# Three attention stages of a two-block transformer kernel: the first scores inside the last projection, transposes four steps behind the scores

## The chip, the core and the metric

The kernel is one program on one core of a Trainium2 chip. The time is the device time of one execution in microseconds (us); the median of the runs of the kernel before is 2651.66 us. The engines are TensorE (PE, with its weight loads as PEld), VectorE (DVE), ScalarE (ACT), GpSimd (POOL) and SyncE (SP, which issues the loads). They run side by side, each in its own program order, and meet through semaphores.

## The reference, cut to what matters

Two blocks run over 512 tokens of width 1024 (16 heads of 64). The change touches three attention stages, called a, b and c here:

```
a: logits = q k / 8 over the keys that an index picked     (causal by blocks)
b: logits = q k / 8 + decay[query] - decay[key]            (causal)
c: logits = norm(q) norm(k) / 8                            (all keys)
p  = softmax(logits)        o = p v        x = x + o @ w_o
```

Around them stand projections (`x @ w_q` and the like), MLPs and a gated MLP, all in float32.

## The kernel before

**Stages.** Everything runs as one chain of matrix products on PE, a projection as tiles of one PSUM bank each (128x512 or 128x256), in banks 0 to 3 in turn. A product splits the operands into a high and a low part and adds three matmuls for each piece (lines 452 to 454, for `va` and `vc` 475 to 477). ACT and POOL split the weights of the next 256 columns ahead of time (`split`, lines 900 and 1706), SP loads them. Between products and the next norm ACT and DVE evacuate each tile. All orders are written out by hand, engine by engine.

**An attention.** There are 32 steps, `STEPS = (c, i)`: pair of heads c (8 of them), query block i (4). In a and b step i is 128(i+1) keys wide, in c always 512. So four steps make a group of a pair. A step n passes these operations:

1. PE, line 584 (in b also 592, for the decay): the scores of the two heads, into banks `2 * (n % 2) + e`.
2. DVE, line 1329 (c: 1327): takes them out of PSUM with the mask and the minimum, into a row of `PA`/`PBB`/`PC` (8 rows, `ROWS`, two for a step).
3. ACT, line 991: exponential and its sum.
4. DVE, line 1342: reciprocal of the two sums; DVE does it for step n - 1 after it has taken the scores of step n.
5. POOL, line 1740, and DVE, line 1345: each row times its reciprocal. Of the even steps DVE takes one row and POOL one, of the odd steps POOL takes both.
6. PE, line 609, `turn`: transposes of both rows into banks 4 and 5; all steps use these two banks, so a turn waits until the copies of the turn before are out.
7. ACT, line 985, and DVE, line 1336: copies of banks 4 and 5 to `TA`/`TB`/`TC` (of the even steps one each, of the odd steps both on ACT).
8. PE, line 624, `values`: the product with v, into bank 6 or 7; after each group ACT and DVE (lines 995, 1349) take it out as the input of the output projection.

The loop over n does the scores of step n, then the turn of step n - 3 (`TURN`), then the values of step n - 5 (`SUM`). Each engine has the same loop with its own share, so what stands ahead in an engine's order delays what stands behind it. ACT does, in its turn n, first the copies of turn n - 3 and then the exponentials of step n; DVE the scores of step n, the copy of turn n - 3, the reciprocals of step n - 1.

**Before and behind.** The first scores wait until the last projection (`va`, `qb`, `vc`) is through and its four banks are free (`wait_bank` of the tiles `end + i`). The products `oa`, `ob`, `oc` follow the last values. The last projection of b, `qb`, has eight tiles of 24 matmuls, that of c, `vc`, four tiles of 24 half as wide.

Of the kernel before, what the change touches and what calls it, by code (L numbers as in the profile page):

```python
# [19 lines left out]

ROWS, TURN, SUM = 8, 3, 5
BIG = 1e30
# [94 lines left out]
def body(nc, ctx, t, consts, out):  # L117
# [223 lines left out]
    def by_heads(x, w):  # L341

        return x.rearrange("p (e k) -> p e k", e=2)[:, :, 0:w // 2]

    def scaled_by(a, n):

        return 16 * ATT[a] + n // 2 + 1, 48 * ATT[a] + n + 1 + (n + 1) // 2

# [39 lines left out]
    def freed(g):  # L388
        return FREED[g]

    def tensor_program(pe):
# [180 lines left out]

        def attend(a, heads_q, heads_k, heads_v):

            base, x0 = 64 * ATT[a], fill_base(a + "o")[1]

            def scores(n):
                c, i = STEPS[n]
                w = width(a, i)  # L580
                for e in range(2):
                    if n >= 2:
                        pe_until.wait_ge(sc_out, base + 2 * n + e - 3)
                    m = pe.matmul(bank[2 * (n % 2) + e][:, 0:w], heads_q(2 * c + e, i), heads_k(2 * c + e, w), start=True, stop=(a != "b"))  # L584
                    if a != "b":
                        m.then_inc(sc_full, 1)
                if a == "b":

                    for e in range(2):  # L590
                        o, h = 64 * e, 2 * c + e
                        pe.matmul(bank[2 * (n % 2) + e][:, 0:w], PICK[o:o + 64, h:h + 1].to_broadcast([64, P]), CK[o:o + 64, 0:w],
                                  start=False, stop=True).then_inc(sc_full, 1)
# [33 lines left out]

            for n in range(len(STEPS) + SUM):
                if n < len(STEPS):
                    scores(n)  # L630
                if TURN <= n < len(STEPS) + TURN:
                    turn(n - TURN)
                if n >= SUM:
                    values(n - SUM)

# [70 lines left out]
        pe_until.wait_ge(key_copy, 4)  # L706
        for i in range(4):
            wait_bank(GEMM["va"].end + i)
        attend("a",
               lambda h, i: QA[64 * (h % 2):64 * (h % 2) + 64, h // 2, i * P:(i + 1) * P],  # L710
               lambda h, w: KA[h // 4][64 * (h % 2):64 * (h % 2) + 64, 0:w],
               lambda h, j: VA[:, j, 64 * (h // 4):64 * (h // 4) + 64])
        fm("oa", X, lambda c: wait_chunk("ao", c))
# [43 lines left out]
        tm_wide("vb", lambda c: wait_chunk("kv", c), after_vb)  # L757
        fm("qb", X, lambda c: wait_chunk("qb", c), first=lambda c: wait_high("qb", c))
        pe_until.wait_ge(ck_dve, 7)
        for i in range(4):  # L760
            wait_bank(GEMM["qb"].end + i)
        attend("b",
               lambda h, i: QB[64 * (h % 2):64 * (h % 2) + 64, h // 2, i * P:(i + 1) * P],
               lambda h, w: KB[64 * (h % 2):64 * (h % 2) + 64, h // 2, 0:w],
               lambda h, j: VB[:, j, 64 * h:64 * h + 64])
        fm("ob", X, lambda c: wait_chunk("bo", c))
# [40 lines left out]
        pe_until.wait_ge(rot_sum, 17)  # L807
        pe_until.wait_ge(key_copy, 8)
        for i in range(4):
            wait_bank(GEMM["vc"].end + i)  # L810
        attend("c",
               lambda h, i: QC[64 * (h % 2):64 * (h % 2) + 64, h // 2, i * P:(i + 1) * P],
               lambda h, w: KCC[h // 4][64 * (h % 2):64 * (h % 2) + 64, 0:w],
               lambda h, j: VC[:, j, 64 * (h // 4):64 * (h // 4) + 64])
        fm("oc", X, lambda c: wait_chunk("co", c))
# [70 lines left out]
    def scalar_program(act):  # L886
# [86 lines left out]

        def attend(a):
            base = 64 * ATT[a]
            for n in range(len(STEPS) + SUM + 1):
                if TURN <= n < len(STEPS) + TURN:
# [180 lines left out]
        def evac_vc(o):  # L1158
# [54 lines left out]
    def vector_program(dve):  # L1213
# [98 lines left out]
        def attend(a, mask):  # L1312
            base, hi0 = 64 * ATT[a], fill_base(a + "o")[0]
            for n in range(len(STEPS) + SUM + 1):
                if n < len(STEPS):
                    i = STEPS[n][1]
                    w = width(a, i)
                    for r in (2 * n, 2 * n + 1):
                        p, st = PROBS[a][r % ROWS], stat[:, r % ROWS, :]
                        b = bank[2 * (n % 2) + r % 2]  # L1320
                        dve_until.wait_ge(sc_full, base + r + 1)
# [15 lines left out]
                if 1 <= n < len(STEPS) + 1:  # L1337
# [359 lines left out]
    def gpsimd_program(pool):  # L1697
# [230 lines left out]
```

## Time and profile before

| | |
|---|---|
| median of 3 runs (lowest, highest) | 2651.66 us (2650.67, 2652.53) |
| the profiled execution | 2654.48 us, its span 2653.2 us |
| busy share of the span, PE / DVE / ACT / POOL | 97% / 49% / 37% / 47% |
| attention a, first scores to the first matmul of `oa` | 147.0 to 224.2 us |
| attention b, first scores to the last values | 783.3 to 861.6 us |
| attention c, first scores to the last values | 1365.8 to 1460.5 us |

PE is busy almost throughout, and the chain of work that ended last lies on it for 84% of the span; so a microsecond in which PE waits, or runs at a lower clock, is a microsecond of the time. A row of the timeline gives start, duration, engine, line, what is written and read, count, and in brackets how long the engine stood idle before and what ended that. Matmul durations overlap their neighbours' (a matmul's start to the next one's start is what it costs). A row of groups gives count, busy us, mean ns of one and idle time before; a row by line gives count: ns least/median/most, first and last start. PEclk is the granted TensorE clock as a share of its full 2.4 GHz; 0.50 is 1.2 GHz.

### The profile page before, as it was taken

What the parts mean: (1) busy time and instruction counts of PE and PEld (TensorE: products, weight loads), DVE (VectorE), ACT (ScalarE), POOL (GpSimd) and SP (SyncE); (2) the same over time, 40 slices, a digit from 0 to 9 for tenths busy, and PEclk for the clock granted to TensorE, in tenths of its full rate; (3) what the DMA queues carried; (4) which work ended last, traced back from release to release, by engine and by line L of the source; (5) the groups of instructions that cost most, each with busy time, mean ns of one, the idle gap of its engine ahead of it and who ended that gap; (6) DMA issues with size and microseconds to landing.
All of it is one profiled execution on the core that took longest, in us unless ns stands there. A gap on an engine that the chain in (4) does not pass through costs nothing.

```text
span 2653.2 us, 33052 instructions
## 1 busy us (share of the span) xinstructions
PE 2579.4 (97%) x13418; PEld 2084.4 (79%) x13418; DVE 1288.4 (49%) x2151; ACT 979.5 (37%) x1620; POOL 1255.2 (47%) x618
## 2 busy tenths in 40 slices
PE   8989999999998999999999999999999999999999
PEld 5667888888776888888766888888788888888887
DVE  4863799842035399992557341222345233431221
ACT  4464423223347332232458342232324222432231
POOL 4865444444447444444468344444343444344442
PEclk9999999999999999999999999999999999999999
DMA  4201555532220366552210233322432222333322
GB/s 145 64 17 49 181 188 182 188 117 75 95 80 2 95 196 198 186 165 96 72 49 2 64 111 96 95 95 80 163 96 83 81 94 80 95 96 95 96 96 79
DMA packets 259436, 274.48 MB, mean 103 GB/s; under 512 B 6869, under 2 KB 249301, under 8 KB 259029
## 3 DMA queue, kind: packets, MB, share of 16 engines
q1 hardware_dynamic: 259284, 272.37, 31.9%
q8 instruction: 106, 1.74, 0.3%
q14 instruction: 46, 0.37, 0.0%
HBM read 270.26 MB, written 2.10 MB: 103 GB/s over the span
## 4 chain that ended last, share of the span: by engine, by line
PE 84%; DVE 8%; POOL 4%; issue 2%; ACT 1%; DMA 0%; SPq 0%; DVEq 0%
PE bank L452 22%; PE bank L453 22%; PE bank L454 22%; DVE acc L1362 2%; PE bank L520 2%; PE bank L522 2%; PE bank L521 2%; PE bank L428 2%; PE bank L429 2%; DVE tmp L1397 2%; PE bank L432 2%; POOL PA L1740 1%; POOL PBB L1740 1%; PE bank L584 1%; PE bank L624 1%
## 5 line engine op out<-in xcount | busy, mean ns | idle before, releaser
L1706 POOL TENSOR_TENSOR wlo<-raw,whi 128x1024 fp32r<-128x1024 f32 (+1 forms) x408 | 988.8, 2445 | 1193.9 <-ACT whi L900 1193.8
L452 PE MATMUL bank<-Xhi,whi 128*128 128x512 f32 (+1 forms) x1616 | 640.4, 396 | 1.4 <-POOL wlo L1706 1.4
L453 PE MATMUL bank<-Xlo,whi 128*128 128x512 f32 (+1 forms) x1616 | 629.9, 390 | 0.0
L454 PE MATMUL bank<-Xhi,wlo 128*128 128x512 f32 (+1 forms) x1616 | 629.1, 389 | 0.0
L900 ACT ACTIVATE whi<-raw 128x1024 fp32r<-128x1024 f32 (+1 forms) x408 | 404.9, 1041 | 570.0 <-PE bank L454 495.6
L452 PE MATMUL bank<-Hhi,whi 128*128 128x512 f32 x1024 | 400.6, 391 | 0.0
L453 PE MATMUL bank<-Hlo,whi 128*128 128x512 f32 x1024 | 398.9, 390 | 0.0
L454 PE MATMUL bank<-Hhi,wlo 128*128 128x512 f32 x1024 | 398.4, 389 | 0.0
L452 PEld LDWEIGHTS bank<-Xhi,whi 128*128 128x128 f32 (+1 forms) x1616 | 302.3, 187 | 73.0 <-issue 8.1
L453 PEld LDWEIGHTS bank<-Xlo,whi 128*128 128x128 f32 (+1 forms) x1616 | 302.4, 187 | 65.0 <-issue 3.2
L454 PEld LDWEIGHTS bank<-Xhi,wlo 128*128 128x128 f32 (+1 forms) x1616 | 302.4, 187 | 65.0
L1362 DVE SCALAR_TENSOR_TENSOR acc<-ada,cond,acc 128x256 f32<-128x256 f32 x336 | 272.6, 811 | 12.0
L1265 DVE SCALAR_TENSOR_TENSOR HT<-bank,MOD,HT 128x512 f32<-128x512 f32 (+1 forms) x99 | 72.2, 734 | 404.3 <-PE bank L454 384.9
L1397 DVE TENSOR_TENSOR tmp<-tmp 128x512 f32<-128x512 f32 x128 | 137.2, 1072 | 235.4 <-ACT tmp L1007 235.4
L1007 ACT ACTIVATE tmp<-bank 128x512 f32<-128x512 f32 x128 | 76.6, 598 | 412.6 <-PE bank L454 400.3
L454 PEld LDWEIGHTS bank<-Hhi,wlo 128*128 128x128 f32 x1024 | 192.3, 188 | 40.3
L452 PEld LDWEIGHTS bank<-Hhi,whi 128*128 128x128 f32 x1024 | 192.2, 188 | 39.9
L453 PEld LDWEIGHTS bank<-Hlo,whi 128*128 128x128 f32 x1024 | 192.3, 188 | 39.1
L1263 DVE TENSOR_TENSOR HT<-bank,HT 128x512 f32<-128x512 f32 (+1 forms) x84 | 54.7, 663 | 167.2 <-PE bank L454 167.2
L1400 DVE TENSOR_TENSOR Hlo<-tmp,Hhi 128x512 fp32r<-128x512 f32 x128 | 120.8, 944 | 14.0 <-DVE tmp L1397 0.9
L943 ACT ACTIVATE held<-HT 128x512 f32<-128x512 f32 (+1 forms) x56 | 32.0, 578 | 178.0 <-DVE HT L1263 103.2
L520 PE MATMUL bank<-whi,Xhi 128*128 128x512 f32 x240 | 94.7, 395 | 0.5 <-POOL wlo L1706 0.5
(269 smaller groups left out, 3146.6 us busy)
## 6 DMA issues: line engine op xcount, KB each, us to landing
ada<-in_ada_w SPq DMA_DIRECT2D x48, 1024.0 KB, 5.3
raw<-in_w_up SPq DMA_DIRECT2D x32, 1024.0 KB, 5.7
raw<-in_w_down SPq DMA_DIRECT2D x32, 1024.0 KB, 5.0
raw<-in_mlp_w_in SPq DMA_DIRECT2D x32, 1024.0 KB, 5.6
raw<-in_mlp_w_out SPq DMA_DIRECT2D x32, 1024.0 KB, 5.2
raw<-in_gmlp_w_in SPq DMA_DIRECT2D x24, 1024.0 KB, 5.0
raw<-in_gmlp_w_out SPq DMA_DIRECT2D x12, 1024.0 KB, 5.0
raw<-in_w_in_a SPq DMA_DIRECT2D x8, 1024.0 KB, 5.2
```

Of the source, the lines that this page charges most:

```text
L452: pe.matmul(b[0:rows, :], whi[s][:, c, j:j + rows], hi[:, c, :], start=(c == 0), stop=False)
L453: pe.matmul(b[0:rows, :], whi[s][:, c, j:j + rows], lo[:, c, :], start=False, stop=False)
L454: m = pe.matmul(b[0:rows, :], wlo[s][:, c, j:j + rows], hi[:, c, :], start=False, stop=(c == KC - 1))
L520: pe.matmul(b[:], Xhi[:, c, q * P:(q + 1) * P], hi[:, k, :], start=(c == 0), stop=False)
L900: act.activation(whi[u % 2][:, c0:c1, 0:k], src[:, c0:c1, 0:k], ACT_F.Copy).then_inc(hi_done, 1)
L1007: act.activation(tmp[v % 2][:], bank[(gm.tile + o) % 4][:], ACT_F.Relu).then_inc(up_q, 1)
L1263: d = dve.tensor_tensor(HT[:, o, at], b[:, at], HT[:, o, at], ALU.add)
L1265: d = dve.scalar_tensor_tensor(HT[:, o, at], b[:, at], gate[:, o:o + 1], HT[:, o, at], ALU.mult, ALU.add)
L1362: dve.scalar_tensor_tensor(a[:], src[:, c, :], cd[:, c:c + 1], a[:], ALU.mult, ALU.add).then_inc(ada_step, 1)
L1397: dve.tensor_tensor(r[:], tmp[v % 2][:], tmp[v % 2][:], ALU.mult).then_inc(up_r, 1)
L1400: dve.tensor_tensor(Hlo[g % 2][:, o, :], r[:], Hhi[g % 2][:, o, :].bitcast(F32), ALU.subtract).then_inc(h_lo, 1)
L1706: pool.tensor_tensor(wlo[u % 2][:, c0:c1, 0:k], src[:, c0:c1, 0:k], whi[u % 2][:, c0:c1, 0:k].bitcast(F32), ALU.subtract).then_inc(lo_done, 1)
```

## The change

`TURN` becomes 4 and `SUM` 6: a step is transposed one step later, its values follow one step later, and the loop has one turn more. `ROWS` becomes 10, so that the probability rows last as long; for the room, six buffers of the index stage before attention a (`RL`) now share the space of `TA`. The scores of steps 0 to 3 go to banks 4 to 7, which no projection tile uses; steps 4 and 5 wait for the projection's last tiles in their banks, and turn 0 and values 0 wait until banks 4 to 7 have been read. In b, steps 0 to 3 stand behind tiles 4 to 7 of `qb`, one each; in c, steps 0 and 1 behind tile 2 of `vc` and steps 2 and 3 behind tile 3. ACT's order changes with it; DVE's and POOL's loops only see `TURN` and `SUM`. In a nothing stands between tiles, but the first scores no longer wait for the tiles of `va`. Of the scaling, now the even steps are POOL's with both rows and the odd ones are shared.

```diff
-ROWS, TURN, SUM = 8, 3, 5
+ROWS, TURN, SUM = 10, 4, 6
-        RL = [sb(f"RL{i}", [P, S], F32, region) for i in range(8)]
+        RL = [TA[i // 2][:, i % 2, :] for i in range(6)] + [sb(f"RL{i}", [P, S], F32, region) for i in range(6, 8)]
+    def score_bank(n, e):
+        return (4 if n < TURN else 0) + 2 * (n % 2) + e
...
             def scores(n):
-                    if n >= 2:
+                    if TURN <= n < TURN + 2:
+                        pe_until.wait_ge(*freed(end - 4 + (score_bank(n, e) - end) % 4))
+                    elif n >= 2:
                         pe_until.wait_ge(sc_out, base + 2 * n + e - 3)
             def turn(n):
-                pe_until.wait_ge(pn_dve, by_dve)
+                if n:
+                    pe_until.wait_ge(pn_dve, by_dve)
+                else:
+                    pe_until.wait_ge(sc_out, base + 6)
             def values(n):
+                if n == 0:
+                    pe_until.wait_ge(sc_out, base + 8)
...
-        for i in range(4):
-            wait_bank(GEMM["va"].end + i)
...
+        def after_qb(o):
+            if o == 4:
+                pe_until.wait_ge(ck_dve, 7)
+                pe_until.wait_ge(*freed(GEMM["qb"].tile))
+            if o >= 4:
+                steps_b(o - 4, o - 3)
+        steps_b(4)
         def after_vc(o):
+            if o == 2:
+                pe_until.wait_ge(rot_sum, 17)
+                pe_until.wait_ge(key_copy, 8)
+                pe_until.wait_ge(qn_root, 1)
+                steps_c(0, 2)
+            if o == 3:
+                steps_c(2, 4)
+        steps_c(4)
...
+        def evac_qb(o):
+            keep_heads("qb", QB)(o)
+            if o >= 4:
+                attend("b", o - 4, o - 3)
-                    if n % 2:
+                    if n % 2 == 0:
                         dve_until.wait_ge(rc_done, base // 2 + n)
                         dve.tensor_scalar(p[:, 0:w], p[:, 0:w], both[:, 0, 2:3], None, ALU.mult).then_inc(pn_dve, 1)
-                for r in (2 * n, 2 * n + 1)[1 - n % 2:]:
+                for r in (2 * n, 2 * n + 1)[n % 2:]:
                     pool.tensor_scalar(p[:, 0:w], p[:, 0:w], st[:, 2:3], None, ALU.mult).then_inc(pn_pool, 1)
```

PE at the end of `qb`, before: the last matmul of the last tile, then the scores (`KB,QB` and, for the decay, `CK,PICK`) of steps 0 to 3, the first turn (`ident,PBB`), and the scores of step 4.

```order
L454 MATMUL bank<-Xhi,wlo 128x512
L584 MATMUL bank<-KB,QB 128x128 x2
L592 MATMUL bank<-CK,PICK 128x128 x2
L584 MATMUL bank<-KB,QB 128x256 x2
L592 MATMUL bank<-CK,PICK 128x256 x2
L584 MATMUL bank<-KB,QB 128x384 x2
L592 MATMUL bank<-CK,PICK 128x384 x2
L584 MATMUL bank<-KB,QB 128x512 x2
L592 MATMUL bank<-CK,PICK 128x512 x2
L609 MATMUL bank<-ident,PBB 128x64 x4
L584 MATMUL bank<-KB,QB 128x128 x2
```

The same place of the changed kernel, from the last matmul of the last tile on (its lines are 5 to 14 further down).

```order
L459 MATMUL bank<-Xhi,wlo 128x512
L595 MATMUL bank<-KB,QB 128x512 x2
L603 MATMUL bank<-CK,PICK 128x512 x2
L595 MATMUL bank<-KB,QB 128x128 x2
L603 MATMUL bank<-CK,PICK 128x128 x2
L623 MATMUL bank<-ident,PBB 128x64 x4
L595 MATMUL bank<-KB,QB 128x256 x2
```

Steps 0 to 2 have gone ahead of it, behind tiles 4, 5 and 6, so only step 3 stands between the last tile and step 4, and the first turn stands behind step 4.

ACT over the last tiles of `qb`, before: the split of weights (`whi<-raw`), two evacuations, then the exponentials (`PBB,stats`) and the first copies of a turn (`TB`).

```order
L900 ACTIVATE whi<-raw 128x1024 x2
L1098 ACTIVATE QB<-bank 128x512 x2
L900 ACTIVATE whi<-raw 128x1024 x2
L1098 ACTIVATE QB<-bank 128x512 x2
L991 ACT_TABLE_LOAD
L991 ACTIVATE PBB,stats<-PBB,stats 128x128 x2
L991 ACTIVATE PBB,stats<-PBB,stats 128x256 x2
L991 ACTIVATE PBB,stats<-PBB,stats 128x384 x2
L985 ACTIVATE TB<-bank 128x2x64
```

The same in the changed kernel.

```order
L926 ACTIVATE whi<-raw 128x1024 x2
L1124 ACTIVATE QB<-bank 128x512
L1017 ACT_TABLE_LOAD
L1017 ACTIVATE PBB,stats<-PBB,stats 128x128 x2
L1124 ACTIVATE QB<-bank 128x512
L1017 ACTIVATE PBB,stats<-PBB,stats 128x256 x2
L926 ACTIVATE whi<-raw 128x1024 x2
L1124 ACTIVATE QB<-bank 128x512
L1017 ACTIVATE PBB,stats<-PBB,stats 128x384 x2
L1124 ACTIVATE QB<-bank 128x512
L1017 ACTIVATE PBB,stats<-PBB,stats 128x512 x2
L1011 ACTIVATE TB<-bank 128x2x64
```

Each evacuation of tiles 4 to 7 has the exponentials of one step behind it, the split of the first weights of `ob` stands behind the exponentials of step 1, and the first copy of a turn behind those of step 3.

POOL at the start of attention b, before: the last weight split, then one row of step 0 (128 wide), both of step 1, one of step 2, both of step 3, one of step 4.

```order
L1706 TENSOR_TENSOR wlo<-raw,whi 128x1024 x8
L1740 TENSOR_SCALAR PBB<-PBB,stats 128x128
L1740 TENSOR_SCALAR PBB<-PBB,stats 128x256 x2
L1740 TENSOR_SCALAR PBB<-PBB,stats 128x384
L1740 TENSOR_SCALAR PBB<-PBB,stats 128x512 x2
L1740 TENSOR_SCALAR PBB<-PBB,stats 128x128
```

The same in the changed kernel.

```order
L1738 TENSOR_TENSOR wlo<-raw,whi 128x1024 x8
L1772 TENSOR_SCALAR PBB<-PBB,stats 128x128 x2
L1772 TENSOR_SCALAR PBB<-PBB,stats 128x256
L1772 TENSOR_SCALAR PBB<-PBB,stats 128x384 x2
L1772 TENSOR_SCALAR PBB<-PBB,stats 128x512
L1772 TENSOR_SCALAR PBB<-PBB,stats 128x128 x2
```

In a and b POOL has lost one of the two widest rows of a group and has both of the 384 wide ones; the number of rows is the same.

## Rows read from the trace of the kernel before

**Rows 1.** PE's waits for POOL in a, b, c: total us, times, longest.

```profile
PE bank L609 <- POOL PA L1740: 8.5, 9, 2.1
...
PE bank L609 <- POOL PBB L1740: 7.5, 9, 2.1
...
PE bank L609 <- POOL PC L1740: 8.7, 9, 1.8
```

**Rows 2.** Timeline of PE, one group of four steps of a (steps 8 to 11).

```profile
162.59 0.49 PE L584 MATMUL bank<-KA,QA 64*128 64x128 f32 x4
163.42 0.47 PE L609 MATMUL bank<-ident,PA 64*128 64x64 f32 x8 [0.34 <-DVE TA L1336]
...
168.05 0.71 PE L609 MATMUL bank<-ident,PA 64*128 64x64 f32 x16 [0.93 <-POOL PA L1740]
...
171.26 0.49 PE L584 MATMUL bank<-KA,QA 64*128 64x128 f32 x4
```

**Rows 3.** Timeline of PE, one group of b (steps 8 to 11).

```profile
798.20 0.49 PE L584 MATMUL bank<-KB,QB 64*128 64x128 f32 x4
...
799.03 0.46 PE L609 MATMUL bank<-ident,PBB 64*128 64x64 f32 x8 [0.28 <-DVE TB L1336]
...
803.66 0.71 PE L609 MATMUL bank<-ident,PBB 64*128 64x64 f32 x16 [0.64 <-POOL PBB L1740]
...
807.11 0.49 PE L584 MATMUL bank<-KB,QB 64*128 64x128 f32 x4
```

**Rows 4.** Timeline of PE, two groups of c (scores of steps 8, 12, 16).

```profile
1384.15 1.13 PE L584 MATMUL bank<-KC,QC 64*128 64x512 f32 x4
...
1394.44 1.13 PE L584 MATMUL bank<-KC,QC 64*128 64x512 f32 x4
1396.29 0.71 PE L609 MATMUL bank<-ident,PC 64*128 64x64 f32 x16 [0.72 <-POOL PC L1740]
...
1405.68 1.13 PE L584 MATMUL bank<-KC,QC 64*128 64x512 f32 x4
```

**Rows 5.** Timeline of PE, the first scores of a, b, c.

```profile
147.04 4.41 PE L584 MATMUL bank<-KA,QA 64*128 64x128 f32 x16 [3.38 <-ACT VA L1081]
...
783.30 0.46 PE L584 MATMUL bank<-KB,QB 64*128 64x128 f32 x3 [0.78 <-ACT QB L1098]
...
1365.82 5.18 PE L584 MATMUL bank<-KC,QC 64*128 64x512 f32 x16 [0.56 <-ACT VC L1164]
```

**Rows 6.** Timeline of PE: last scores (step 31), then `oa` or the last values.

```profile
212.65 1.13 PE L584 MATMUL bank<-KA,QA 64*128 64x512 f32 x4
...
224.17 0.50 PE L452 MATMUL bank<-Xhi,whi 128*128 128x512 f32 x1
...
849.45 1.13 PE L584 MATMUL bank<-KB,QB 64*128 64x512 f32 x4
...
857.77 3.85 PE L624 MATMUL bank<-TB,VB 128*64 128x128 f32 x36
...
1448.03 1.13 PE L584 MATMUL bank<-KC,QC 64*128 64x512 f32 x4
...
1457.70 2.84 PE L624 MATMUL bank<-TC,VC 128*64 128x128 f32 x48
```

**Rows 7.** Windows: length, busy PE, PEld, DVE, ACT, POOL (count), PEclk, DMA.

```profile
155.00:160.00 5.00, 4.83 (x38) 2.79 (x36) 2.07 (x8) 2.76 (x8) 4.45 (x5) 0.50 0.00 0
...
170.00:180.00 10.00, 8.73 (x116) 6.09 (x114) 6.72 (x28) 8.48 (x29) 8.29 (x8) 1.00 0.01 2
...
790.00:795.00 5.00, 4.83 (x46) 3.49 (x46) 3.14 (x12) 2.70 (x11) 3.88 (x5) 0.50 0.01 3
```

**Rows 8.** Durations: an exponential of c; POOL's scaling, b by form, c by line.

```profile
1368.57 0.70 ACT L991 ACTIVATE PC<-PC,stats 128x512 f32<-128x512 f32 x1
...
L1740 POOL TENSOR_SCALAR PBB<-PBB,stats 128x384 f32<-128x384 f32 x8 | 11.6, 1454 | 6.1 <-DVE stats L1342 6.1
...
L1740 POOL TENSOR_SCALAR PC<-PC,stats x48: 1560/1566/1859, 1370.0 to 1455.4; 128x512 f32<-128x512 f32 x48
```

More of the change, by code:

```diff
@@ L343, in by_heads @@
         return x.rearrange("p (e k) -> p e k", e=2)[:, :, 0:w // 2]
+    def score_bank(n, e):
+        return (4 if n < TURN else 0) + 2 * (n % 2) + e
     def scaled_by(a, n):
-        return 16 * ATT[a] + n // 2 + 1, 48 * ATT[a] + n + 1 + (n + 1) // 2
+        return 16 * ATT[a] + (n + 1) // 2, 48 * ATT[a] + n + 2 + n // 2
     def turned_by(a, r):
@@ L572, in rotation, with attention @@
             pe.matmul(bank[4][0:rows, :], perm[p][0:rows, 0:rows], rotated(r)[0:rows, :], start=True, stop=True).then_inc(rot_full, 1)
-        def attend(a, heads_q, heads_k, heads_v):
+        def attention(a, last, heads_q, heads_k, heads_v):
             base, x0 = 64 * ATT[a], fill_base(a + "o")[1]
+            end = GEMM[last].end
             def scores(n):
@@ L581, in scores @@
                 for e in range(2):
-                    if n >= 2:
+                    if TURN <= n < TURN + 2:
+                        pe_until.wait_ge(*freed(end - 4 + (score_bank(n, e) - end) % 4))
+                    elif n >= 2:
                         pe_until.wait_ge(sc_out, base + 2 * n + e - 3)
-                    m = pe.matmul(bank[2 * (n % 2) + e][:, 0:w], heads_q(2 * c + e, i), heads_k(2 * c + e, w), start=True, stop=(a != "b"))
+                    m = pe.matmul(bank[score_bank(n, e)][:, 0:w], heads_q(2 * c + e, i), heads_k(2 * c + e, w), start=True, stop=(a != "b"))
                     if a != "b":
@@ L591, in scores @@
                         o, h = 64 * e, 2 * c + e
-                        pe.matmul(bank[2 * (n % 2) + e][:, 0:w], PICK[o:o + 64, h:h + 1].to_broadcast([64, P]), CK[o:o + 64, 0:w],
+                        pe.matmul(bank[score_bank(n, e)][:, 0:w], PICK[o:o + 64, h:h + 1].to_broadcast([64, P]), CK[o:o + 64, 0:w],
                                   start=False, stop=True).then_inc(sc_full, 1)
@@ L626, in values, with steps @@
                 m.then_inc(pv_done, 1)
[L628 to L634, printed above, removed]
+            def steps(first, to=len(STEPS) + SUM):
+                for n in range(first, to):
+                    if n < len(STEPS):
+                        scores(n)
+                    if TURN <= n < len(STEPS) + TURN:
+                        turn(n - TURN)
+                    if n >= SUM:
+                        values(n - SUM)
+            return steps
         pe_until.wait_ge(ident_in, 16)
@@ L706, in tensor_program @@
         pe_until.wait_ge(key_copy, 4)
-        for i in range(4):
-            wait_bank(GEMM["va"].end + i)
[L709 to L712, printed above, removed]
+        attention("a", "va",
+                  lambda h, i: QA[64 * (h % 2):64 * (h % 2) + 64, h // 2, i * P:(i + 1) * P],
+                  lambda h, w: KA[h // 4][64 * (h % 2):64 * (h % 2) + 64, 0:w],
+                  lambda h, j: VA[:, j, 64 * (h // 4):64 * (h // 4) + 64])(0)
         fm("oa", X, lambda c: wait_chunk("ao", c))
@@ L757, in tensor_program @@
         tm_wide("vb", lambda c: wait_chunk("kv", c), after_vb)
[L758 to L765, printed above, removed]
+        steps_b = attention("b", "qb",
+                            lambda h, i: QB[64 * (h % 2):64 * (h % 2) + 64, h // 2, i * P:(i + 1) * P],
+                            lambda h, w: KB[64 * (h % 2):64 * (h % 2) + 64, h // 2, 0:w],
+                            lambda h, j: VB[:, j, 64 * h:64 * h + 64])
+        def after_qb(o):
[4 more added lines that the diff above has]
+                steps_b(o - 4, o - 3)
+        fm("qb", X, lambda c: wait_chunk("qb", c), after_qb, first=lambda c: wait_high("qb", c))
+        steps_b(4)
         fm("ob", X, lambda c: wait_chunk("bo", c))
@@ L800, in tensor_program @@
         fm("qc", X, lambda c: wait_chunk("c", c), after_qc)
+        steps_c = attention("c", "vc",
+                            lambda h, i: QC[64 * (h % 2):64 * (h % 2) + 64, h // 2, i * P:(i + 1) * P],
+                            lambda h, w: KCC[h // 4][64 * (h % 2):64 * (h % 2) + 64, 0:w],
+                            lambda h, j: VC[:, j, 64 * (h // 4):64 * (h // 4) + 64])
         def after_vc(o):
@@ L805, in after_vc @@
                 rotation(ROT_C_AT["q", 7], 1)
-        tm("vc", lambda c: wait_chunk("c", c), after_vc)
[L807 to L814, printed above, removed]
+            if o == 2:
[5 more added lines that the diff above has]
+                steps_c(2, 4)
+        tm("vc", lambda c: wait_chunk("c", c), after_vc)
+        steps_c(4)
         fm("oc", X, lambda c: wait_chunk("co", c))
@@ L972, in copy_keys, with attend @@
                 act.activation(k[64:128, :], k[0:64, :], ACT_F.Copy).then_inc(key_copy, 1)
-        def attend(a):
+        def attend(a, first=0, to=len(STEPS) + SUM + 1):
             base = 64 * ATT[a]
-            for n in range(len(STEPS) + SUM + 1):
+            for n in range(first, to):
                 if TURN <= n < len(STEPS) + TURN:
@@ L1123, in scalar_program @@
         fill("qb", None, GEMM["vb"].end)
-        units("qb", keep_heads("qb", QB))
-        attend("b")
+        def evac_qb(o):
+            keep_heads("qb", QB)(o)
+            if o >= 4:
+                attend("b", o - 4, o - 3)
+        units("qb", evac_qb)
+        attend("b", 4)
         units("ob", lambda o: square("ob", GEMM["ob"].tile + o, o))
@@ L1164, in evac_vc @@
             act.activation(VC[:, o, :], bank[g % 4][:, 0:256], ACT_F.Copy).then_inc(copied, 1)
+            if o == 2:
+                attend("c", 0, 2)
         units("vc", evac_vc)
-        attend("c")
+        attend("c", 2)
         units("oc", lambda o: square("oc", GEMM["oc"].tile + o, o))
@@ L1319, in attend @@
                         p, st = PROBS[a][r % ROWS], stat[:, r % ROWS, :]
-                        b = bank[2 * (n % 2) + r % 2]
+                        b = bank[score_bank(n, r % 2)]
                         dve_until.wait_ge(sc_full, base + r + 1)
```

## The prediction

> **What bounds the kernel now.** The chain of waits lies on PE for 84% of the span, so I looked only for time that PE loses in a, b and c: by waiting, or at a lower clock. The list of PE's waits came first: in each attention PE waits nine times for POOL before a turn, 24.7 us in all [rows 1]. The timelines then show three kinds of places.
>
> *The middle* (steps 8 to 31, six groups). A group of a takes 171.26 - 162.59 = 8.67 us, of which PE waits 0.34 for DVE's copy of the turn before and 0.93 for POOL, so its work is 7.4 [rows 2]. A group of b takes 8.91, waits 0.28 + 0.64 = 0.92, work 8.0 [rows 3]. In c four steps without a wait take 10.29, the next four 11.24, so one wait of 0.72 costs 0.95 [rows 4]; five such follow steps 8 to 31. Clock: 1.00 there, with ACT busy 8.48 of 10 us in a [rows 7].
>
> *The head* (end of the last projection tile to the scores of step 8). In b it runs from 783.30 - 0.78 = 782.52 to 798.20, 15.7 us [rows 3, 5]; in a from 143.66 to 162.59, 18.9 [rows 2, 5]; in c from 1365.26 to 1384.15, 18.9 [rows 4, 5]. PE's work in a head is eight scores, turns 0 to 4, values 0 to 2. Start to next start, a group's work (the 13, 18 and 12 rows between the first and last of rows 2, 3 and the first two of rows 4) splits into scores 2.9, 3.5, 3.9; turns 1.7, 1.7, 2.4; values 2.8, 2.8, 4.1 for a, b, c. That makes 5.8 + 1.9 + 1.8 = 9.5 (a), 7.0 + 1.9 + 1.8 = 10.7 (b), 7.8 + 2.9 + 3.1 = 13.8 (c). Lost: 9.4, 5.0, 5.1. Part of it in a and b is the clock at 0.50 behind the idle stretches [rows 7].
>
> *The tail* (scores of step 31 to the last values): 11.5, 12.2 and 12.5 us [rows 6]. Its work is one score, four turns, six values: 1.0 + 1.7 + 4.6 = 7.3; 1.2 + 1.7 + 4.6 = 7.5; 1.0 + 2.4 + 6.1 = 9.5. Lost: 4.2, 4.7, 3.0.
>
> **The change part by part.** It takes no matmul away. Each score, turn and value still costs PE the same, wherever it stands; what can be won is lost time, 9.4 + 5.0 + 5.1, 7.6 + 5.5 + 4.75, and 4.2 + 4.7 + 3.0, together 49. So I ask at each place what is late next.
>
> *Middle.* A turn one step later gives the chain behind the scores (DVE, ACT, DVE, POOL) one more step, 1.85 to 2.6 us, against waits of at most 0.93: the POOL waits go, if POOL is not full. It is not: in a and b a group's rows now cost 2 x 0.61 + 0.93 + 2 x 1.45 + 1.56 = 6.6 (means of the same view as the 1454 of [rows 8]; one 512 row fewer than before, one 128 and one 384 more than the 256 and 512 given up), in c 6 x 1.6 = 9.6 of 10.3. DVE's wait goes too: the copy of the 128 wide turn now stands behind two 128 wide scores instead of two 512 wide ones. Next is ACT: at its share in [rows 7] it needs 7.35 us a group in a, PE 7.4. ACT copies turn 3 of a group only after the exponentials of step 2 and the evacuation of the finished pair, and turn 0 waits for that copy. Laying a group's operations side by side gives about 0.2 there and 0.1 at the next turn, so 7.7 instead of 8.67: 5.8 us in six groups (between 0, if ACT's order gives back all, and 7.6). In b PE needs 0.6 more and ACT no more, and I find no wait: 5.5 (3 to 5.5). In c, PE 10.3 against ACT's two exponentials of 0.70 and one and a half copies a step, no wait: 4.75 (0.5 to 4.75). Sum 16.05.
>
> *Head of b.* Scores 0 to 2 disappear under `qb`: DVE had nothing there, ACT one copy a tile, and the weight split of `ob` that now waits for the exponentials of step 1 has the whole attention as cover; without that cover it would cost some 3 us. After the last tile PE does scores 3 and 4, turn 0, scores 5; then turn 1 waits for the copy of turn 0, which ACT does behind the exponentials of step 3 (two scores off PSUM, 2 x 0.70 of exponentials): about 1.3 us. Turn 2 waits for POOL's two 384 wide rows, 2.9 us [rows 8], whose reciprocal DVE issues behind the scores of step 3: about 0.65. Lost 2.0 instead of 5.0, **gain 3.0** (0.5 with the clock down again, 5 with no wait). *Head of c.* Scores 0 and 1 run before the last tile; their operands are ready by then. Behind it the four scores 2 to 5 come faster than DVE and ACT pass them at 1.4 us a step, and the copy of turn 0 stands behind the exponentials of step 3: about 2.1, and 0.6 at the turns behind. Lost 2.7 instead of 5.1, **gain 2.4** (1 to 5). *Head of a.* The first scores wait for the key copies alone, 0.7 us earlier; 2.7 of idle stays. Waits as in b, 2.0, and I leave one half-clock stretch in, 1.7. Lost 6.4 instead of 9.4, **gain 3.0** (0.7 to 4.8). Sum 8.4.
>
> *Tail.* Behind step 31 now stand five turns and seven values, so PE has 1.2 to 1.6 us more to do while step 31 passes the other engines, and of its two 512 wide rows POOL has one instead of two, 1.56 us less [rows 8]. Left are the copy of turn 28 behind the exponentials of step 31 and a rest at turn 31: lost 1.7 (a), 1.6 (b), 0.5 (c). Gains 2.5 + 3.1 + 2.5 = 8.1 (4.5 to 11).
>
> *At nothing:* the shared buffers of the index stage (read before attention a starts), the two more rows, the turn of the loop (no new operation). They would cost a wait at 147 if POOL's index sums still ran there; POOL had been idle.
>
> Sum: 16.05 + 8.4 + 8.1 = 32.5. The profiled execution, 2654.48, is 2.8 above the median; it would give 2622.0, the median 2651.66 - 32.5 = **2619.2**.
>
> **The rivals.** *ACT takes POOL's place.* In a and b ACT's order returns half of what the middle and all heads gain: 5.65 + 4.75 + 4.2 + 8.1 = 22.7, so 2629. For it: 8.48 of 10 us busy at 8.67 a group. Against: in c ACT has slack and the steps without a wait run at 2.57 now.
>
> *POOL is stretched.* A POOL row of c takes 1560 ns at least and 1859 at most [rows 8], the long ones beside a DVE scaling. DVE's rows are now the wide ones. If every row took 0.3 more, c's POOL would need 6 x 1.86 = 11.15 a group (gain 0.5), a and b 8.4 (gains 1.6 and 3.0): 5.1 + 16.5 = 21.6, so 2630. 
>
> *The clock goes down again* in the heads of b and c, two stretches like that of 790 to 795: 3.4 each, so 2626.
>
> *Nothing moves:* the waits reappear one step later since an engine, not the order, is full: only part of the tails, about 2648.
>
> *Slower.* The middle of b falls to 1.2 GHz: its work of 8.0 a group doubles, 48 us in six groups, so 2667; it decides from some 76 us of the 250 at the lower level (half of it is lost, against 32.5 + 5.3). For it: 790 to 795 ran at 0.50 with PE busy 4.83 of 5 [rows 7]. Against: the middle of a, as full of transposes and gaps, has 1.00. The Trainium skill, "TensorE: Matmul & The Clock Gate", Part 4, says that transposes do not count as activity for the clock the way matmuls do; with 1.7 of 8.67 us in transposes at 1.00, the trace does not show it at this share.
>
> **How the numbers follow.** Forecast 0.62, ACT 0.16, POOL 0.08, clock in the heads 0.06, nothing moves 0.04, slower 0.04. The range 2612 to 2634 takes in the forecast with its bounds and the middle of the next three. Faster by over 0.2% (5.3 us, about what a measurement tells from no change) 0.92, within 0.2% 0.04, slower 0.04.
>
> **What would show it.** PE's waits for POOL: nearly none in the middles. Groups of 7.7, 8.0 and 10.3 us. In b PE idle for under 2.5 us between the last tile of `qb` and step 8, at a clock of 1.00, and waits at turn 1 put down to ACT or DVE. Tails with under 2 us idle. It is wrong if groups of a stay above 8.2, if the waits carry POOL's name still, or if the clock is down in the middle.

## The result, and the profile after

The changed kernel takes 2628.87 us (median of 4 runs, 2627.30 to 2630.21) against 2651.16 (4 runs, 2649.05 to 2652.53): a ratio of 0.9918 [0.9904, 0.9931], 22.3 us less. Forecast were 2619.2, 32.5 less. The profiled executions are 2654.48 and 2627.30, 27.2 apart; the one of before lies some 3 us above its median.

The view of PE's waits, whole span (who waits <- for whom: total us, times, longest), the rows of the attentions:

```profile
PE bank L623 <- ACT TA L1011: 7.3, 14, 1.7
PE bank L623 <- ACT TB L1011: 5.6, 14, 1.7
...
PE bank L595 <- ACT KA L998: 2.7, 1, 2.7
PE bank L623 <- DVE TC L1368: 2.4, 1, 2.4
...
PE bank L623 <- ACT TC L1011: 1.2, 3, 0.7
PE bank L623 <- POOL PA L1772: 1.2, 3, 0.6
...
PE bank L623 <- POOL PC L1772: 0.2, 1, 0.2
PE bank L623 <- DVE TB L1368: 0.2, 1, 0.2
PE bank L623 <- POOL PBB L1772: 0.2, 1, 0.2
```

POOL's 24.7 us [rows 1] are 1.6. In c nothing has come in their place but 3.8 us, all of them in the head and the tail. In a and b ACT's copies of the turns, which did not stand among the waits of before with any weight, have 12.9 us.

The timeline of PE, a group of a (answers rows 2), then of b (rows 3):

```profile
164.21 0.49 PE L595 MATMUL bank<-KA,QA 64*128 64x128 f32 x4
165.00 0.34 PE L623 MATMUL bank<-ident,PA 64*128 64x64 f32 x4 [0.30 <-ACT TA L1011]
...
167.18 0.46 PE L623 MATMUL bank<-ident,PA 64*128 64x64 f32 x8 [0.41 <-ACT TA L1011]
...
172.43 0.49 PE L595 MATMUL bank<-KA,QA 64*128 64x128 f32 x4
```

```profile
792.24 0.49 PE L595 MATMUL bank<-KB,QB 64*128 64x128 f32 x4
792.98 0.34 PE L623 MATMUL bank<-ident,PBB 64*128 64x64 f32 x4 [0.19 <-ACT TB L1011]
...
795.10 0.46 PE L623 MATMUL bank<-ident,PBB 64*128 64x64 f32 x8 [0.23 <-ACT TB L1011]
...
800.65 0.49 PE L595 MATMUL bank<-KB,QB 64*128 64x128 f32 x4
```

And of c, the scores of steps 8 and 12:

```profile
1360.92 1.13 PE L595 MATMUL bank<-KC,QC 64*128 64x512 f32 x4
...
1371.21 1.13 PE L595 MATMUL bank<-KC,QC 64*128 64x512 f32 x4
```

A group of a takes 172.43 - 164.21 = 8.22 us (before 8.67), one of b 8.41 (8.91). But the first group behind the head, which has no finished pair to evacuate, takes 7.67 in a (156.54 to 164.21) and 7.97 in b, just the forecast. In c every group takes 10.29, without a wait (rows 4 of before: 11.24). What holds a and b is seen on the other two engines, here in a (DVE, then ACT, a group later):

```profile
171.17 0.35 DVE L1377 TENSOR_SCALAR PA<-PA,stats 128x256 f32<-128x256 f32 x1
172.15 0.69 DVE L1381 TENSOR_TENSOR Xlo<-bank,Xhi 128x512 fp32r<-128x512 f32 x1 [0.62 <-ACT Xhi L1021]
172.75 0.68 DVE L1361 CUSTOM_DVE_ANT_0 PA<-bank,MA 128x512 f32<-128x512 f32 x1
```

```profile
171.53 0.58 ACT L1021 ACTIVATE Xhi<-bank 128x512 fp32r<-128x512 f32 x1
172.01 1.08 ACT L1011 ACTIVATE TA<-bank 128x512 f32<-128x512 f32 x2
173.48 0.72 ACT L1017 ACTIVATE PA<-PA,stats 128x512 f32<-128x512 f32 x1 [0.39 <-DVE stats L1361]
...
174.91 0.25 ACT L1011 ACTIVATE TA<-bank 128x128 f32<-128x128 f32 x1
```

The output of a finished pair of heads leaves PSUM in two parts: ACT writes `Xhi`, DVE then subtracts it for `Xlo`. DVE comes to `Xlo` at 171.53, just as ACT, behind its exponentials, starts `Xhi`; it stands there for the 0.62 us of `Xhi` and takes the 512 wide scores only at 172.75, though PE had started writing them at 170.18. On ACT the copies of the 512 wide turn stand behind `Xhi` (172.01 to 173.09). Then ACT idles 0.39 us for DVE's scores, its exponentials end late, and behind them stands the copy of the 128 wide turn (174.91). PE waits once for the first of these copies and once for the second, in the group above 0.30 and 0.41 us. The first wait is there without a pair too, with 0.24 us.

Where the time went, by parts of an attention in the profiled executions. Head: from ACT's first evacuation of a tile of the product ahead (`VA`, `QB`, `VC`) to the scores of step 8, so that scores between tiles count wherever they stand. Middle: steps 8 to 31. Tail: from the scores of step 31 to the first matmul of the output product.

| us, before -> after | a | b | c |
|---|---|---|---|
| head | 28.38 -> 22.57 | 50.16 -> 46.23 | 29.23 -> 25.25 |
| middle | 50.06 -> 46.56 | 51.25 -> 47.63 | 63.88 -> 59.18 |
| tail | 11.52 -> 11.20 | 12.10 -> 12.08 | 12.44 -> 12.31 |
| all | 89.96 -> 80.33 | 113.51 -> 105.94 | 105.55 -> 96.74 |

Together 309.0 -> 283.0, so 26.0 of the 27.2 us lie here. The cut moves work: a turn and a product with v of the head (0.27 + 0.80 us in a and b, 1.6 in c, from the timeline) now follow in the tail (1.2 and 1.6). In time lost, as the prediction counted, the heads gained 4.7 + 2.9 + 2.4 = 10.0, the middles 11.8, the tails 1.5 + 1.2 + 1.7 = 4.4. Forecast were 8.4, 16.05 and 8.1.

### The profile page after: what moved, and what is told of

Same layout as the page of the kernel before. It is cut to its first block, busy times and chain, and to the rows that moved or that the text cites. A ratio compares the mean times of both kernels' runs of the same rounds, so it can differ in the third digit from the quotient of the medians.

```text
span 2626.0 us, 33091 instructions
## 1 busy us (share of the span) xinstructions
PE 2568.1 (98%) x13418; PEld 2077.3 (79%) x13418; DVE 1290.3 (49%) x2151; ACT 979.4 (37%) x1620; POOL 1244.5 (47%) x618
## 3 DMA queue, kind: packets, MB, share of 16 engines
q8 instruction: 106, 1.74, 0.3%
## 4 chain that ended last, share of the span: by engine, by line
PE 87%; DVE 7%; ACT 2%; issue 2%; POOL 1%; DMA 0%; SPq 0%; DVEq 0%
PE bank L457 22%; PE bank L458 22%; PE bank L459 22%; DVE acc L1394 2%; PE bank L640 2%; PE bank L525 2%; PE bank L527 2%; PE bank L526 2%; PE bank L595 2%; PE bank L433 2%; DVE tmp L1429 2%; PE bank L434 2%; PE bank L437 1%; PE bank L623 1%; DVE Hlo L1432 1%
```

## The experiments

Theory: the step of slack took POOL's waits away; what came in their place in a and b is the *place* of the pair's evacuation in the engines' orders. Rival: ACT is *full* there, as its busy time suggests (8.94 of 10 us in the window 170 to 180, before 8.48 [rows 7]; columns as there).

```profile
170.00:180.00 10.00, 9.29 (x120) 5.93 (x117) 7.47 (x32) 8.94 (x29) 8.08 (x10) 1.00 0.01 2
```

All medians stand against runs of the kernel before on the same chip (medians of 2650.3 to 2651.2 us). "Slot" names the turn of an engine's loop at whose end the evacuation stands, by the width of the step whose scores (DVE) or exponentials (ACT) that turn does, ahead of the evacuation; the groups are those of the steady middle.

| kernel | slot ACT / DVE | group a / b / c, us | three attentions | median, ratio |
|---|---|---|---|---|
| before (turn 3, values 5) | 256 / 256 | 8.67 / 8.91 / 11.23 | 309.0 | |
| changed (turn 4, values 6) | 384 / 384 | 8.23 / 8.41 / 10.29 | 283.0 | 2628.87, 0.9918 |
| evacuation two turns later | 128 / 128 | 7.66 / 7.97 / 10.29 | 276.1 | 2620.08, 0.9882 [0.9869, 0.9896] |
| evacuation one turn later | 512 / 512 | 9.20 / 9.52 / 11.68 | 304.8 | 2646.86 (one run) |
| values 5 behind | 256 / 256 | 8.62 / 8.73 / 11.68 | 297.7 | 2642.00, 0.9968 [0.9957, 0.9980] |
| parts apart | 384 / 128 | 7.73 / 7.97 / 10.29 | 275.8 | 2621.03, 0.9888 [0.9874, 0.9901] |
| parts apart, ACT later | 512 / 128 | 8.13 / 8.46 / 10.29 | 283.2 | 2630.22, 0.9922 [0.9908, 0.9935] |
| extra copy ahead | 128 / 128 | 8.14 / 8.15 / 10.54 | 280.6 | 2626.32 (one run) |
| extra copy behind | 128 / 128 | 7.78 / 8.02 / 10.29 | 276.5 | 2619.83 (one run) |
| no scores between tiles | 384 / 384 | 8.23 / 8.41 / 10.29 | 285.4 | 2630.82, 0.9923 [0.9911, 0.9936] |
| old share of the scaling | 384 / 384 | 8.17 / 8.35 / 10.59 | 284.7 | 2628.05, 0.9911 [0.9898, 0.9925] |
| turns 3 behind, new share | 256 / 256 | 9.02 / 9.02 / 11.43 | 308.0 | 2656.70, 1.0021 [1.0012, 1.0030] |
| turns 3 behind, old share | 256 / 256 | 8.67 / 8.91 / 11.23 | 303.1 | 2648.30, 0.9994 [0.9985, 1.0002] |

**The evacuation two turns later.** In ACT's and DVE's loops alone (the last pair stays where it was):

```diff
-                if n > SUM and (n - SUM) % NT == 0:
-                    c = (n - SUM) // NT - 1
+                c = pair_at(n)      # (n - SUM - 2) % NT == 0
+                if c is not None:
```

> The changed kernel with the evacuation of a finished pair (ACT's Xhi, DVE's Xlo) two turns of the loop later, behind the 128 wide step and no longer behind the 384 wide one. Order theory: in a and b this pair of operations stands ahead of DVE's scores and ACT's exponentials of the widest step and makes a group 8.23 instead of 7.67 us (a) and 8.41 instead of 7.97 us (b). Then five groups of each fall back to 7.7 and 8.0, PE's waits for ACT in the middles go, c stays at 10.29: 5 x 0.56 + 5 x 0.43 = 5 us less than the changed kernel, about 2624. Rival, ACT is full: ACT does the same work in a group, so groups stay at 8.2 and 8.4 with the wait at another turn, 2629.

Measured: 2620.08 us, 8.8 less than the changed kernel's median, and the intervals of the two ratios lie apart; groups 7.66, 7.97, 10.29. The gain is larger than the 5 us expected since the tails shrink too (11.20 -> 10.36, 12.08 -> 10.50, 12.31 -> 11.91; some 0.9 us of b's is clock, see below). The groups are those of the order theory, the time is below both forecasts. DVE still waits, but ahead of 256 wide scores and not of 512 wide ones:

```profile
177.21 0.69 DVE L1388 TENSOR_TENSOR Xlo<-bank,Xhi 128x512 fp32r<-128x512 f32 x1 [0.73 <-ACT Xhi L1028]
177.82 0.41 DVE L1368 CUSTOM_DVE_ANT_0 PA<-bank,MA 128x256 f32<-128x256 f32 x1
```

**Values five steps behind.** One constant of the change undone, which moves the slot one turn earlier:

```diff
-ROWS, TURN, SUM = 10, 4, 6
+ROWS, TURN, SUM = 10, 4, 5
```

> One constant of the change undone: the values follow five steps behind the scores and not six, the turns stay four behind. The evacuation of a finished pair then stands one turn of the loop earlier, behind the 256 wide step and ahead of the 384 wide one, as in the kernel before. Order theory: what costs 0.56 us (a) and 0.43 us (b) a group is the place ahead of the widest step; groups of a 7.7, of b 8.0, as with the later evacuation, c 10.3. The tails have one product with v less as cover for the last copies, 0 to 0.5 us each; 2620 to 2623. Rival: any place ahead of a step of 384 or more costs the same, groups stay at 8.2 and 8.4, 2628 to 2631.

Measured: neither; all groups are slower, c by 1.4 us, and the time is 2642.00. The theory "ahead of the widest step" was too simple. The list of waits names DVE's copies, 22.4 us over heads, middles and tails:

```profile
PE bank L623 <- DVE TC L1368: 9.3, 7, 2.4
...
PE bank L623 <- DVE TA L1368: 7.8, 7, 1.2
...
PE bank L623 <- DVE TB L1368: 5.3, 7, 0.8
```

DVE copies a part of the even turns only, and with turns four steps behind it does that in the even turns of its loop. An evacuation at the end of an odd turn of the loop stands right ahead of the next even turn's scores and copy, for which PE waits; before, with turns three behind, those copies fell into the odd turns of the loop. So, as long as the evacuation's place follows from `SUM`, `TURN` and `SUM` have to move together, as the change did.

**The evacuation one turn later** (the same edit with 1 for 2), the other odd slot.

> The evacuation of a pair one turn of the loop later than in the changed kernel, behind the widest step's exponentials and ahead of the 128 wide step. Order theory: the widest step no longer waits for it, but the copies of the 128 wide turn do; groups of a 7.7 to 8.0, of b 8.0 to 8.2. Rival, ACT is full: 8.2 and 8.4 as in the changed kernel.

Measured: 9.20, 9.52, 11.68, a miss for both, with the same waits (DVE's copies, 9.7 + 9.2 + 8.6 us). How long DVE stands there, from its own waits between 164 and 200 us of a (the kernels in the order: changed, values five behind, one turn later):

```profile
DVE Xlo L1381 <- ACT Xhi L1021: 3.1, 5, 0.6
```

```profile
DVE Xlo L1381 <- ACT Xhi L1021: 6.1, 4, 1.5
```

```profile
DVE Xlo L1388 <- ACT Xhi L1028: 8.4, 4, 2.1
```

0.6, 1.5 and 2.1 us a group, ahead of scores in the first and of scores and a copy in the others.

**The parts apart.** ACT's part where the changed kernel has it, DVE's two turns later, so that DVE finds it ready:

```diff
-                c = pair_at(n)
+                c = pair_at(n, 0)   # ACT; DVE: 2
```

> The changed kernel with ACT's part of the evacuation where it was (behind the 384 wide step's exponentials) and DVE's part two turns of the loop later, so that DVE never stands waiting for it. Theory, DVE's place in the queue: what costs 0.56 and 0.43 us a group is DVE waiting 0.6 us for ACT and then working 0.6 us ahead of the widest scores; groups are 7.4 to 7.7, 8.0 and 10.29, 2619 to 2622. Rival, ACT's own order: the copy stands ahead of ACT's two widest copies of a turn still, groups stay at 8.1 to 8.2 and 8.3 to 8.4, 2627 to 2629.

Measured: 2621.03 us; groups 7.73, 7.97, 10.29, and no wait of DVE for `Xhi` is left in that stretch. A group of a on PE:

```profile
165.51 0.49 PE L602 MATMUL bank<-KA,QA 64*128 64x128 f32 x4
...
173.23 0.49 PE L602 MATMUL bank<-KA,QA 64*128 64x128 f32 x4
```

Nine tenths of the loss in a and all of it in b are DVE's place; ACT's own order costs at most the 0.06 us by which 7.73 exceeds 7.67. This is the run that settles the middle.

**The parts apart, ACT one turn later** (1 for ACT, 2 for DVE).

> The same, with ACT's part one turn later (behind the widest step's exponentials, the copy of the 128 wide turn behind it) and DVE's part one turn after that, behind the 128 wide step. By the theory of DVE's place groups are 7.5 to 7.8, 8.0 and 10.29, as DVE finds the pair ready; 2618 to 2622. By the rival, ACT's own order, the copy of the 128 wide turn comes 0.5 us later and the next turn waits for it in each group of a and b: 8.0 and 8.3, 2625.

Measured: 2630.22; groups 8.13 and 8.46, the numbers of the rival, although DVE does not wait for `Xhi` here either. ACT's copy of the 128 wide turn now stands behind `Xhi` and ends at 175.86; PE's next turn, which comes soonest behind that copy, starts 0.25 after it, 0.38 late:

```profile
175.10 0.59 ACT L1028 ACTIVATE Xhi<-bank 128x512 fp32r<-128x512 f32 x1
175.58 0.28 ACT L1018 ACTIVATE TA<-bank 128x128 f32<-128x128 f32 x1
...
176.11 0.46 PE L630 MATMUL bank<-ident,PA 64*128 64x64 f32 x8 [0.38 <-DVE PA L1384]
```

(The trace puts the wait down to DVE's scaling, whose row a later turn needs; of what this turn needs by the code, the copy is the last row ahead of it.) So each engine has its bad slots; ACT's slot behind the 384 wide step is a good one.

**An extra copy, ahead and behind.** Is ACT full? The kernel with the evacuation two turns later, with one more 128x512 copy a group on ACT, first ahead of `Xhi`, then behind it:

```diff
+                    act.activation(Xlo[:, c, :], bank[6 + c % 2][:], ACT_F.Copy)
                     act.activation(Xhi[:, c, :], bank[6 + c % 2][:], ACT_F.Copy).then_inc(x_hi, 1)
```

> The kernel with the later evacuation, and ACT takes each finished pair out of PSUM twice (one more 128x512 copy of 0.58 us a group, into a buffer that DVE then overwrites). Order theory: there is room for it at this place, behind the 128 wide step: groups of a 7.7 to 7.95, of b 8.0, of c 10.29. Rival, ACT is full: a group takes the whole 0.58 more in a and about half in b: 8.2 and 8.25.

```diff
                     act.activation(Xhi[:, c, :], bank[6 + c % 2][:], ACT_F.Copy).then_inc(x_hi, 1)
+                    if c + 1 < KC:
+                        act_until.wait_ge(x_hi, fill_base(a + "o")[0] + c + 1)
+                        act.activation(Xlo[:, c + 1, :], Xhi[:, c, :].bitcast(F32), ACT_F.Copy)
```

> The kernel with the later evacuation, with one more 128x512 copy on ACT a group as in the run before, but behind the evacuation and not ahead of it, so that DVE gets the pair as early as without it. If the 0.48, 0.18 and 0.25 us a group that the extra copy cost in a, b and c came over DVE (it stands waiting for the pair 0.5 us longer), groups are 7.7 to 7.8, 8.0 and 10.3. Rival, ACT is full: the same price wherever the copy stands, 8.1, 8.15, 10.5.

Measured: ahead, 8.14, 8.15 and 10.54, by the rival's numbers in a; behind, 7.78, 8.02 and 10.29, so 0.12, 0.05 and 0 for a copy of the same size (it reads `Xhi` and not PSUM, and takes 0.63 us in place of 0.59). ACT's busy time in the window 170 to 200 of a (columns as in rows 7) is higher in the faster one (ahead, then behind):

```profile
170.00:200.00 30.00, 27.86 (x354) 17.96 (x348) 22.84 (x94) 27.79 (x88) 22.91 (x23) 1.00 0.01 2
```

```profile
170.00:200.00 30.00, 28.94 (x378) 19.69 (x376) 23.42 (x95) 29.38 (x94) 24.61 (x23) 1.00 0.01 2
```

With ACT 29.38 of 30 us busy the extra copy costs PE 0.12 a group; with ACT 27.79 us busy it costs four times that, as DVE stands 1.2 us for `Xhi` in place of 0.7. ACT was not full in the changed kernel, whose operations fit into groups of 7.66 us two turns later; the rival falls.

**No scores between tiles.** All steps of b and c behind the last tile, the banks as in the change:

```diff
-                steps_b(o - 4, o - 3)
-        steps_b(4)
+        steps_b(0)
...
-                steps_c(0, 2)
-                steps_c(2, 4)
-        steps_c(4)
+        steps_c(0)
```

> The changed kernel without the scores between projection tiles: all steps of b and c start behind the last tile, still in the other banks. What the heads of b and c gain by the interleaving goes back: by the prediction 3.0 + 2.4 = 5.4 us, of which the other banks keep some 1 us, so 4 to 6 us above the changed kernel, 2633 to 2635, with the middles unchanged. Rival, the turns wait for the same chain wherever the scores start: the same time as the changed kernel, 2629.

Measured: 2630.82. The intervals of the ratios overlap, so by the time alone the interleaving is not told from nothing. In the profiled executions the heads of b and c are 47.30 and 26.74 against 46.23 and 25.25: worth 1.1 + 1.5 = 2.6 us, half of the 5.4. Part of it is the clock: without the interleaving a stretch at 0.50 stands in each of the two heads (774 to 779 and 1350 to 1356, both at 0.93) where the changed kernel has 1.00. The rest of these heads' gain comes with the turns' later place: with turns three behind and the old share of the scaling (the next experiment), the same interleaving and banks give 0.7 + 1.9 us.

**Turns three behind,** with the new share of the scaling and with the old one, all else as changed:

```diff
-ROWS, TURN, SUM = 10, 4, 6
+ROWS, TURN, SUM = 8, 3, 5
```

> The changed kernel with the turns three steps behind the scores and the values five (8 rows), as before; the interleaving, the banks and the new share of the scaling stay. Theory: the step of slack is what took POOL's waits away, so the middles are back at 8.7, 8.9 and 11.2 us a group and most of the tails too, and only the heads' gain is left: some 15 to 20 us above the changed kernel, 2644 to 2649. Rival, the new share of the scaling took POOL's waits away (POOL has one 512 wide row in a group instead of two): groups of a and b stay near 8.2 and 8.4, c near 10.3 to 10.8, 2631 to 2636.

> Only the scores between the projection's tiles and their banks: turns three and values five steps behind as before, scaling shared as before. If the slower groups of the run with turns three behind (9.0, 9.0, 11.4 us) came from the new share of the scaling, groups are back at 8.67, 8.91 and 11.23, and the time is that of the kernel before less the 2 us that the interleaving is worth: 2649. Rival: the interleaving itself costs something when the turns follow three behind (a lower clock, or the first turn in front of the last tile's evacuation): 2653 or more with groups as before.

Measured: 2656.70 with the new share, slower than before and than both forecasts, and 2648.30 with the old one, where groups are those of before to 0.02 us and PE's waits for POOL are back:

```profile
PE bank L622 <- POOL PA L1771: 9.2, 9, 2.1
...
PE bank L622 <- POOL PC L1771: 6.9, 7, 1.8
PE bank L622 <- POOL PBB L1771: 6.4, 8, 2.1
```

The step of slack is what cured POOL; the rival (the new share did it) falls. The new share alone costs 7.8 us when turns follow three behind (5.6 above its runs of before against 2.1 below them; 4.9 in the attentions of the profiled executions): PE then waits 1.03 us for DVE's copy in each group of a (0.34 before [rows 2]). The interleaving and the banks without the slack are worth 2.1 us at the median, with an interval that holds zero.

**The old share of the scaling,** turns four behind:

```diff
-                    if n % 2 == 0:
+                    if n % 2:
...
-                for r in (2 * n, 2 * n + 1)[n % 2:]:
+                for r in (2 * n, 2 * n + 1)[1 - n % 2:]:
```

> The changed kernel with the share of the scaling as before (even steps shared by DVE and POOL, odd steps both rows on POOL). Theory: with four steps between scores and turns POOL is in time either way in the middles; only the tails and the end of the heads see it, as POOL has two 512 wide rows of step 31: 0.5 to 1.5 us in each of three attentions, 2630 to 2633. Rival, the share is needed: PE's waits for POOL come back once in a group of a and b, 2637 or more.

Measured: 2628.05, the same time, and less than the 1.5 to 4.5 us that the theory had put on it. The middle of c loses 1.7 us (60.92 against 59.18), those of a and b gain 0.4 and 0.3, and the tail of a is 0.35 longer. With the slack, the new share is worth nothing that shows.

## Why the prediction was right, and where its sum was not

**Right: the sign, the range, the cause.** POOL's waits went, because of the later turns (the two runs with turns three behind); POOL was not full and not stretched further, the rows of c take 1557 at least, 1563 in the median and 1855 ns at most, as before [rows 8]. In the heads turn 1 waits for the copy of turn 0 and turn 2 a little for POOL, as said, with 1.74, 1.67 and 2.42 us against 1.3, 1.3 and 2.1 (a, b, c):

```profile
152.02 0.46 PE L623 MATMUL bank<-ident,PA 64*128 64x64 f32 x8 [1.74 <-ACT TA L1011]
...
153.52 0.59 PE L623 MATMUL bank<-ident,PA 64*128 64x64 f32 x12 [0.34 <-POOL PA L1772]
...
779.52 0.46 PE L623 MATMUL bank<-ident,PBB 64*128 64x64 f32 x8 [1.67 <-ACT TB L1011]
...
781.01 0.59 PE L623 MATMUL bank<-ident,PBB 64*128 64x64 f32 x12 [0.16 <-POOL PBB L1772]
...
1354.73 0.71 PE L623 MATMUL bank<-ident,PC 64*128 64x64 f32 x16 [2.42 <-DVE TC L1368]
```

**Wrong: the middles of a and b, 5.8 + 5.5 forecast, 3.5 + 3.6 measured.** The failed step is "laying a group's operations side by side gives about 0.2 there and 0.1 at the next turn", and in b "I find no wait". It followed ACT past the evacuation and left out DVE's half of it, which waits for ACT's and stands ahead of the 512 wide scores. By its own test ("wrong if groups of a stay above 8.2") the middle of a was wrong by a hair, 8.23. The rival "ACT takes POOL's place" gave 2629, which is the time; but its reason, an engine nearly full, is not what the runs show. Its price was an assumption (half of it comes back) that happened to fit, and its parts are not the measured ones: heads of 4.2 against 10.0, tails of 8.1 against 4.4.

**Wrong: the tails, 8.1 forecast, 4.4 measured.** The failed step is "of its two 512 wide rows POOL has one instead of two, 1.56 us less". POOL's last three rows of a took 4.55 us before and 4.16 after: for the 512 wide row given up it has a second 384 wide one. And they start later behind the scores of step 31, since the evacuation of the seventh pair now stands ahead of these on DVE. The timeline of a, before (DVE's first row of step 31, POOL's last three, PE's last turn), then after (the same between PE's scores of step 31 and its last turn):

```profile
213.81 0.69 DVE L1329 CUSTOM_DVE_ANT_0 PA<-bank,MA 128x512 f32<-128x512 f32 x1 [0.76 <-PE bank L584]
...
215.49 4.55 POOL L1740 TENSOR_SCALAR PA<-PA,stats 128x384 f32<-128x384 f32 x3 [0.52 <-DVE stats L1342]
...
220.10 1.12 PE L609 MATMUL bank<-ident,PA 64*128 64x64 f32 x16 [2.08 <-POOL PA L1740]
```

```profile
203.10 1.13 PE L595 MATMUL bank<-KA,QA 64*128 64x512 f32 x4
...
205.68 0.68 DVE L1361 CUSTOM_DVE_ANT_0 PA<-bank,MA 128x512 f32<-128x512 f32 x1
...
207.16 4.16 POOL L1772 TENSOR_SCALAR PA<-PA,stats 128x384 f32<-128x384 f32 x3 [1.92 <-DVE stats L1374]
...
211.42 0.72 PE L623 MATMUL bank<-ident,PA 64*128 64x64 f32 x16 [0.63 <-POOL PA L1772]
```

From PE's start on step 31 to DVE's it was 213.81 - 212.65 [rows 6] = 1.16 us and is 2.58; to the last turn it was 7.45 and is 8.32, of which 1.2 is moved work. So the chain through step 31 sets the tail, and the waits of 0.73 and 1.04 us for ACT's copies ahead of it lie in its shadow. With the 0.63 at the last turn PE idles 2.4 us, and the prediction's own sign, "under 2 us idle", fails here. With the evacuation two turns later DVE follows PE after 1.27 us, and the tail is 10.36.

Much of what the tails of a and b did gain is clock, which the prediction's account of the tails does not name. Before, both have a stretch at 0.50 behind PE's wait of 2.08 us for POOL (220 to 224 and 857 to 861, at 0.62): from the last turn to the output product PE took 4.07 and 4.42 us there and takes 2.88 and 2.89 now, so 1.2 and 1.5 us of gain. In b some 0.9 us goes back: the window 835 to 844 of the changed kernel has 0.81, a stretch that the run without interleaving does not have (tail 11.20 against 12.08).

**Wrong on the good side: the head of a, 3.0 forecast, 4.7 measured.** The half-clock stretch that I left in, 1.7 us, did not come: 155 to 160, at 0.50 before [rows 7], is at 1.00:

```profile
155.00:160.00 5.00, 4.75 (x72) 3.58 (x70) 3.75 (x18) 4.80 (x18) 5.00 (x7) 1.00 0.00 2
```

The run with turns three behind and the old share has 0.99 there and a head of 25.00 against 28.38, so part of this gain belongs to that one execution of before, and with it to the 3 us by which it lies over its median. The term of 1.7 was too large in any case: the eight other kernels with turns four and values six behind do have such a stretch there (their heads of a have a mean clock of 0.93, the changed kernel 1.00), and these heads take 22.72 to 23.43 us, 0.2 to 0.9 more than 22.57. The rival that cost most, a lower clock in the middle of b, did not come: the middles of all thirteen kernels are at 1.00, also with groups of 7.66 us of which 1.7 are transposes, but for one stretch in a. With the evacuation one turn later, 168 to 172 is at 0.61 behind a wait of 1.46 us for DVE's copy, and that group takes 10.65 us where the others take 9.20. (The Trainium skill, "TensorE: Matmul & The Clock Gate", Part 4, has it that transposes do not count as activity the way matmuls do; at this share no run here shows a cost of it.)

**Wrong: the median taken for the profiled execution.** The parts gained 26.2 us between the two profiled executions, the medians 22.3. The prediction read what one execution of before lost, half-clock stretches and all, and took it whole off the median, though that execution lay 2.8 us above it. So of the 10.2 us by which 32.5 was too much, 6.3 are in the parts, and 3.9 lie between this pair of executions and the medians; which operations they belong to no run shows.

## What to carry to other kernels

An operation that two engines do one after the other (one writes the high part, the other subtracts) stalls the second in its own order for as long as the first is queued; cost both places, and what stands behind each, or put the second part a turn later. When offsets of a hand-written pipeline move, lay the rare operations (once in four steps here) beside the frequent ones by parity and width: the same evacuation cost between 0 and 1.5 us a group by its slot alone. That an engine is 90% busy says little of its price: 0.58 us more on ACT cost 0.48 us ahead of a wait and 0.12 behind it.

## What the runs showed of the hardware that was not expected

The granted clock at one place differs between executions of kernels that do much the same work there. In the window 151 to 156, in a's head, it is 0.84 before, 1.00 in the changed kernel and 0.66 with turns three behind and the old share, where 155 to 160 is then at 0.99 and not at 0.50. The changed kernel and the one without scores between tiles do the same in a, and their heads take 22.57 and 23.27 us, with 146 to 151 at 1.00 and 0.66. So a microsecond or so of a head in a single profiled execution is the clock's and not the change's. The cause was not looked for.
